# Order of the weight loads in the expert loop of a hybrid encoder layer: gate of the expert two ahead in front of up and down

## The reference

```python
u = rmsnorm(h, ffn_norm[l])
# hier_moe: top-1 of 4 groups, top-2 of the 8 experts in it
for gi in range(N_GROUPS):
    sl = slice(gi * EXPERTS_PER_GROUP, (gi + 1) * EXPERTS_PER_GROUP)
    hg = jnp.einsum('nd,edf->nef', t, w_gate[sl])
    hu = jnp.einsum('nd,edf->nef', t, w_up[sl])
    hid = jax.nn.silu(hg) * hu * comb[:, sl, None]
    out = out + jnp.einsum('nef,efd->nd', hid, w_down[sl])
...
return rmsnorm(h, final_norm)[:, N_META:]
```

## Time and profile before

| | |
|---|---|
| median of 3 runs | 1552.65 us (1552.53 to 1552.84) |
| span of the profiled execution, first to last instruction | 1549.8 us |
| its own time beside the span | not listed apart; the median lies 2.85 us over the span |
| TensorE busy, share of the span | 1521.5 us, 98% |
| VectorE, ScalarE, GpSimd busy | 514.0, 222.5, 55.7 us |
| DMA moved | 479.60 MB, mean 309 GB/s |
| granted TensorE clock, mean | 0.999 of full speed |

### The profile page before, as it was taken

The page is one execution under the profiler, slowest core; times in us unless marked ns, Lnnn a source line. Parts: engine busy times, 40 slices in busy tenths (PEclk is TensorE's granted clock), DMA queues, the critical chain, the costliest instruction groups (busy, mean ns, idle before and its releaser), DMA issues.

```text
span 1549.8 us, 23417 instructions
## 1 busy us (share of the span) xinstructions
PE 1521.5 (98%) x10075; PEld 978.1 (63%) x10075; DVE 514.0 (33%) x1113; ACT 222.5 (14%) x485; POOL 55.7 (4%) x58
## 2 busy tenths in 40 slices
PE   9999999999999999999999999999999999999997
PEld 6888777778876445656556556556556556556553
DVE  2566348743583104121321321321321321321323
ACT  3002313222312203000000000000000000000003
POOL 0000121003020000000000000000000000000000
PEclk9999999999999999999999999999999999999999
DMA  9743332141236046999999999999999999999996
GB/s 349 239 160 109 110 110 88 50 166 46 89 110 272 0 175 259 380 402 420 409 430 434 432 426 435 427 430 435 432 425 434 427 431 435 432 425 430 431 430 255
DMA packets 61084, 479.60 MB, mean 309 GB/s; under 512 B 10561, under 2 KB 19282, under 8 KB 41042
## 3 DMA queue, kind: packets, MB, share of 16 engines
q1 hardware_dynamic: 60736, 478.55, 75.0%
q10 hardware_dynamic: 290, 0.23, 0.1%
HBM read 476.66 MB, written 2.10 MB: 309 GB/s over the span
## 4 chain that ended last, share of the span: by engine, by line
PE 70%; DMA 23%; DVE 4%; ACT 1%; issue 1%; POOL 0%; SPq 0%; DVEq 0%; ACTq 0%; POOLq 0%
PE bank L1094 21%; DMA ring<-in_w_up_dram 21%; PE bank L758 20%; PE bank L909 7%; PE bank L1119 7%; PE bank L1174 4%; PE bank L1052 3%; DMA ring<-in_w_down_dram 2%; DVE region_m L1729 1%; PE bank L847 1%; PE bank L827 1%; PE bank L674 1%; PE bank L850 0%; PE bank L856 0%; PE bank L1112 0%
## 5 line engine op out<-in xcount | busy, mean ns | idle before, releaser
L1094 PE MATMUL bank<-ring,region_m 128*64 128x256 f32 x4096 | 455.7, 381 | 7.0 <-DMA ring<-in_w_up_dram 7.0
L1094 PEld LDWEIGHTS bank<-ring,region_m 128*64 128x64 f32 x4096 | 290.6, 137 | 162.6 <-issue 12.6
L758 PE MATMUL bank<-region_u,ring 128*128 128x272 f32 (+2 forms) x1536 | 369.6, 393 | 0.0
L758 PEld LDWEIGHTS bank<-region_u,ring 128*128 128x128 f32 x1536 | 283.8, 190 | 52.3 <-issue 0.9
L1119 PE MATMUL bank<-region_qy,region_s 128*64 128x512 f32 x992 | 218.4, 592 | 0.5 <-issue 0.5
L1119 PEld LDWEIGHTS bank<-region_qy,region_s 128*64 128x64 f32 x992 | 71.8, 137 | 127.8 <-issue 119.1
L1964 DVE TENSOR_TENSOR region_s<-region_s,bank 128x256 f32<-128x256 f32 x32 | 13.5, 421 | 334.5 <-PE bank L1094 334.5
L1052 PEld LDWEIGHTS bank<-region_m,region_u 128*128 128x128 f32 x960 | 108.3, 192 | 11.7 <-issue 11.7
L1174 PE MATMUL bank<-region_m 128*128 128x512 f32 x256 | 114.1, 599 | 0.0
L1052 PE MATMUL bank<-region_m,region_u 128*128 128x128 f32 x960 | 111.2, 277 | 0.0
L1729 DVE SCALAR_TENSOR_TENSOR region_m<-region_qy,cols,region_m 128x256 f32<-128x256 f32 x240 | 106.7, 508 | 1.7 <-DVE region_qy L1757 0.5
(11 more groups left out here) (273 smaller groups left out, 823.0 us busy)
## 6 DMA issues: line engine op xcount, KB each, us to landing
ring<-in_w_gate_dram SPq DMA_DIRECT2D x31, 4096.0 KB, 32.7
region_qy<-in_w_down_dram SPq DMA_DIRECT2D x62, 2048.0 KB, 19.9
ring<-in_w_up_dram SPq DMA_DIRECT2D x28, 4096.0 KB, 21.8
ring<-in_w_in_dram SPq DMA_DIRECT2D x40, 1024.0 KB, 7.3
ring<-in_w_up_dram SPq DMA_DIRECT2D x8, 2048.0 KB, 10.5
ring<-in_w_out_dram SPq DMA_DIRECT2D x12, 1024.0 KB, 5.3
ring<-in_w_in_dram SPq DMA_DIRECT2D x16, 512.0 KB, 5.0
region_qy<-in_w_out_dram SPq DMA_DIRECT2D x4, 1024.0 KB, 13.0
```

Source lines behind the costliest of these rows:

```text
L758: last = mm(banks[n % 2][:, 0:width], slot[s][:, 512 * k + P * j:512 * k + P * (j + 1)], uT[:, 4 * g + k, T - width:T], start=g == k == 0, ...
L1094: last = mm(banks[is_up][CAP * i:CAP * (i + 1), 0:FE // 2], uTe[:, k, CAP * x_:CAP * (x_ + 1)], w[:, c0:c0 + FE // 2], start=k == 0, stop= ...
```

## The change

Only the list on SP is reordered. No load, wait or instruction is added or taken away, and no other engine's program changes. In `stream` each gate load moves in front of the up load and the down load that stood ahead of it. In the list written out by hand, down of 1 moves in front of up of 2, gate of 4 in front of up of 3, and gate of 5 in front of up of 4. The loads of the other round (line 652) use the same `stream`.

```diff
             def stream(e, u):
+                load_gate(e, 2, u, 0)
                 load_up(e, 1, u)
                 load_d(e, 0, u)
-                load_gate(e, 2, u, 0)
+                load_gate(e, 3, u, 1)
                 load_up(e, 2, u)
                 load_d(e, 1, u)
-                load_gate(e, 3, u, 1)
...
             load_up_in_halves(1)
             load_gate(0, 3, 0, 1)
+            load_d(0, 1, 0)
             load_up_in_halves(2)
-            load_d(0, 1, 0)
+            load_gate(2, 2, 2, 0)
             load_up_in_halves(3)
             load_d(2, 0, 2)
-            load_gate(2, 2, 2, 0)
+            load_gate(2, 3, 2, 1)
             load_up_in_halves(4)
             load_d(2, 1, 2)
-            load_gate(2, 3, 2, 1)
             with sp.Fori(4, NE - 3, 2) as e:
                 stream(e, e)
```

## The result

| | before | after |
|---|---|---|
| time, median (lowest to highest, 19 runs each) | 1552.47 (1550.64 to 1553.56) | 1555.44 (1553.43 to 1557.42) |
| span of the profiled execution | 1549.8 | 1553.9 |

The ratio is 1.0021, 95% interval 1.0015 to 1.0027: slower by 2.3 to 4.2 us, where +3.8 us was forecast. (The median before is here that of 19 runs, 0.2 us under the one of the three runs shown first.) It is a small number, and it is the difference of two larger ones, so the size alone would not show that the reasons were right. The trace does for some of them.

A forecast was written before the change was run, and what follows sets the result against it. TensorE sets the pace to 1050 us, then the DMA queue, which decides the end. An extra load (+9.7), empty queue won back (-5.0) and the tail (-0.9) give +3.8 us: 1556.4 us, range 1552.8 to 1560.0.

The forecast's parts named there:

- Which part bounds: Expert loop: DMA is slower than TensorE by 0.5 us per expert; without waits the span falls by 7.5 + 0.9 us.
- One more load ahead of up of 30, +9.7: End of loop: gate 31 now stands ahead of up of 30 in the queue, one more 4 MB load, 9.74 us.
- Empty queue won back, 5.0: Start of loop, 645 to 800 us: of 6.3 us of empty queue, 5.0 us are won back (bounds 3.7 to 6.3).
- The gates: Start of loop: four gates issued only 4.4 to 5.7 us ahead still lose 1.3 us of queue (bounds 0 and 2.6).
- The lag of 2.1 us in the landings: Up of 1 to up of 8: 2.1 us of the 8.4 lost are late landings in a deep queue, not won back.
- The tail, -0.9: After up of 30: waits of 0.59 us at up of 31 and 0.34 at the last half of down of 31 go.
- The wait at up 2: Start of loop: TensorE stands about 0.4 us for up of 2's second half, hidden since the DMA sets up of 30.
- Where the waits begin: Expert loop: waits for up begin near 850 us instead of 1072; idle time on up rises from 7.0 to about 12 us.
- The sum: Whole kernel: +9.7 - 5.0 - 0.9 = +3.8 us, span 1553.6, time 1556.4 us; chance 0.48.
- (1): Rival, no measurable change: the lag is empty queue or gates find the queue full; times 1553.1 to 1555.2 us; chance 0.37.
- (2): Rival, faster: with a gate always in hand the loop's queue moves 435 GB/s, 8.5 us less, 1547.9 us; chance 0.06.
- (3): Rival, slower: shallow queue costs 0.64 us at ten gates, 6.4 us lost instead of 1.3, 1561.5 us; chance 0.09.

The follow-up runs named there:

- e1: Kernel before with only the last turn of the loop (e = 28) in the new order; 1.0063 of before, +9.8 us.
- e10: Hand-written list in the new order, loop from e = 4 in the old order; 1.0008 of the kernel before, +1.2 us.
- e4: Hand-written list (experts 0 to 4) in the old order, loop in the new order; 1.0043 of the kernel before, +6.7 us.
- e6: Changed kernel with half the columns of each down matrix's first half, except the last matrix, not loaded (11 MB per expert); 0.9961 of the kernel before, -6.1 us.
- e3: Changed kernel with the new order up to the turn e = 10 and the old order from e = 12; 0.9990 of the kernel before, -1.6 us.
- e2: Changed kernel with only the last turn of the loop (e = 28) in the old order; 1554.61 us, 1.0013 of the kernel before, +2.0 us.
- e7: Kernel before with each up from expert 1 loaded in two halves, the first released 3.5 us earlier; 1.0006 of before, +0.9 us.
- e9: New order to e = 10, old from e = 12, ups in halves, second half of down 1's load behind up 2; 0.9975 of the kernel before, -3.9 us.

## Why the prediction was right, step by step

- **Which part bounds.** Right: with 11 MB per expert no wait for a load is left in the old order and 8.2 us go, where 7.5 + 0.9 were laid out.
- **One more load ahead of up of 30, +9.7.** Right, and shown alone by e1 (one wait 9.7 us longer). The pace stayed at 29.23 us per expert. Up of 30 starts at 1484.9 on before's clock, where 1486 was forecast and under 1483 would have spoken against the empty queue.
- **Empty queue won back, 5.0.** The term is real: in e10 the queue is outright empty when the gate is held back, and in e4 the time is not won back. Its size is settled only to 1.5 us. Up of 30 starts 3.5 us later than before, so 9.7 - 3.5 = 6.2 us were won against the profiled execution before; against e1's, which was 1.5 us ahead with the same list, 4.7. By bytes, 428 GB/s instead of 413 from 645 to 800 is 155 x 15/430.6 = 5.4.
- **The two parts of that term.** The gates: 155 x (1 - 428/430.6) = 0.9 us of queue are still empty, where 1.3 were laid out (about 427 GB/s were forecast), close enough. The lag of 2.1 us in the landings, said to stay: not borne out. After the change up of 2 to up of 8 land 1.5 us later than 17 loads in a full queue would, which is 0.6 more than the bytes have, and in e1 the lag is 7.2 - 6.7 = 0.5. So most of it belonged to the one execution from which it was read, and no run here shows that it comes from the depth of the queue.
- **The tail, -0.9.** From the start of up of 30 to the end of the span it is 68.4 us before and 67.1 after, so 1.3. No wait stands at up of 31 or the last down, as said.
- **The wait at up 2.** 0.86 us instead of 0.4, covered by the queue in the changed kernel; it shows as a cost of 0.8 us in e6.
- **Where the waits begin.** Wrong by three to four experts: up of 12 at 960 us, where I said near 850. In this execution up of 30 came 1.2 us earlier than forecast and the wait at up 2 was 0.5 us longer; that is 1.7 us of margin, and the margin shrinks by 29.2 - 28.7 = 0.5 per expert, so three experts. The idle time on up is 9.4 us, not 12. A shift of three experts is also what e1 shows against before with the same list.
- **The sum.** +9.7 - 6.2 - 1.3 = +2.2 us in the loop, where +3.8 was forecast (the 6.2 is itself read off the two profiles, so this is no check of it). The profiled span is 4.1 longer only because 1.94 us of it lie ahead of the loop. The ratio's +3.3 (2.3 to 4.2) holds the forecast of 3.8, and the loop's 2.2 lies just under it. That the span was forecast at 1553.6 and came out at 1553.9 is luck: 1.94 us of the start made up for what the loop fell short.
- **The rivals.** (1) is not excluded: the lag on which it turned is mostly gone, the loop's +2.2 lies within its +0.4 to +2.5, and the ratio, over 0.2% by a hair, doesn't exclude 0.15%. (2) is out: the rate is 431 GB/s from 800 to 1480 as before. The Trainium skill's rule in "DMA: Bandwidth & Descriptors", section "Rules for kernel authors", to issue early and wait late, holds for the start of this loop (428 GB/s instead of 413) and not for its end, where the early gate stands ahead of a load that is needed sooner (the wait of 10.2 us in e1). (3) is out: it had 6.4 us of empty queue, and by bytes 0.9 us are left to 800 us and none after.

## What to carry to other kernels

When one queue feeds buffers that free at different times, its order does two jobs: the load that can be issued early keeps the queue from running dry, and the load that is needed soonest must not stand behind it. Write the ledger of the queue (what is ahead of the last load that anything waits for, less the time the queue stands empty) before moving a load. In this kernel the prefetch that paid at the start of the loop was worth handing back once the queue was deep without it, and before the consumer started to wait (e3, the one place of return tried there, 1.6 us under before, 0.2 to 2.9); handed back at the last turn it gave nothing that can be measured (e2), handed back too early it was lost in one gap (e10). And a term of a microsecond or two that is read from one execution may belong to that execution: look for it in a second one with the same list.

## What the runs showed of the hardware

A wait of TensorE can cost more than its length. After 10.2 us of standing still the next product, 7.13 us at full clock, took 9.56 (granted clock 0.73 to 0.75), and after 1.97 us in e3 another took 8.79 (0.66). After 1.97 us in e10 and 1.86 us in e4 the next product ran at full clock (3.67 us for half an up, and 7.13 for a whole one), so the length of the wait alone doesn't decide it. The same drop makes executions differ by up to about 3 us ahead of the loop: 16 products took 3.55 us instead of 1.97 near 12 us, and 24 took 4.55 instead of 2.92 near 612 us. Within the loop, loads of the same list landed 1.5 us apart in two executions. So for a change of 0.2% loop lengths are compared from a common event, not spans, and even they only to about 1.5 us. With up loaded as two loads of 2 MB an expert of 12 MB takes 29.29 us in a full queue instead of 29.22 (e7; the waits in e9 are 29.3 us apart too).
